# Third block's attention with tokens taken column by column, three key tiles a query block, both heads in one slot

## The chip, the cores and the metric

The kernel runs on one core of a Trainium2 chip. The metric is the device time of one execution in microseconds (us), lower is better. Five engines take part: TensorE (PE, with its weight loads PEld), VectorE (DVE), ScalarE (ACT), GpSimd (POOL) and SyncE (SP), which only issues DMAs here.

## The reference, cut to what matters

Three blocks run one after another on x of shape (1, 1024, 1024), in float32. The change lies in the third. Its attention sees the 1024 tokens as a grid of 16 rows by 64 columns, token t at row t // 64 and column t % 64. Each query attends to 8 rows by 16 columns around it, clipped at the edges, with a learned bias for each relative place; there are 8 heads of 64 channels.

```python
def neighbourhood_attention(q, k, v, rpb):
    rows = T // GRID_W                       # 16
    kh = min(MAX_KH, rows)                   # 8
    row_start = jnp.clip(row_ids - kh // 2, 0, rows - kh)
    col_start = jnp.clip(col_ids - KW // 2, 0, GRID_W - KW)      # KW 16, GRID_W 64
    ...
        s = jnp.einsum("bhwd,bhiwjd->bhwij", q_row, k_win).astype(jnp.float32) * scale
        s = s + bias.transpose(0, 2, 1, 3).astype(jnp.float32)[None]
        p = jax.nn.softmax(s.reshape(B, N_HEADS, GRID_W, kh * KW), axis=-1)
        return jnp.einsum("bhwij,bhiwjd->bhwd", p, v_win)

def third_block(...):
    proj = rms_norm(h, ln_g[l]) @ w_in[l] + b_in[l]
    glu_a, glu_b, z_conv, q, k, v, z_att = jnp.split(proj, cuts, axis=-1)
    y_conv = conformer_conv(glu_a, glu_b, ...)       # 31 taps along the tokens
    y_att = neighbourhood_attention(q, k, v, rpb[l])
    y_conv = grouped_rms_norm(y_conv, gn_conv_g[l], CONV_GROUPS) * jax.nn.silu(z_conv)
    y_att = grouped_rms_norm(y_att, gn_att_g[l], N_HEADS) * jax.nn.silu(z_att)
    h = h + jnp.concatenate([y_conv, y_att], axis=-1) @ w_out[l]
```

## The kernel before, in words

Activations are kept transposed: channels on the 128 partitions, the 1024 tokens (TOK) along the free axis. A product with a weight block is made of three matmuls (high parts by high, high by low, low by high); one block of 8 weight tiles on 1024 tokens is 48 matmuls (`feature_block`). GpSimd splits each weight block into its two parts ahead of TensorE, two blocks deep. Every result of TensorE goes through one of two PSUM slots `acc[0]` and `acc[1]` of 1024 numbers each, used in turn: `claim` makes TensorE wait until the slot's last reader has counted up `acc_free`.

The order on each engine is written out by hand; the engines meet only at semaphores. The attention of the third block is four units, one for each pair of heads (`near_tensor`, `near_scalar`, `near_vector`). In a unit TensorE makes q, turns v to token-major (`turn_tiles`), makes k and z, adds the rows of the pair before to the residual h (`near_rows`: eight products, each added to h by VectorE in `add_rows`), waits until both slots are free, and enters `att_tensor`. ScalarE takes v, q, k and z out of PSUM (`take`, L1831). VectorE carries the 31-tap convolution of four channel tiles beside it: 23 taps of 1024 tokens a unit (`conv_taps`, L1733), 12 before the gate of the last pair's output and 11 after `near_lo`. `near_hi` (L483 in `split_near`) stands in ScalarE's queue behind the takes of q and of v.

`att_tensor` runs over eight blocks p of 128 queries. Scores of a block are q times the keys that the block may see, for the two heads (sides) of the pair. VectorE adds the bias and takes the maximum (L813, in `att_vector`), ScalarE takes the exponential with its sum (L854), VectorE multiplies by the reciprocal (L823, L826), TensorE turns the probabilities (L720), ScalarE copies them back to SBUF (L864, and L870 for the fifth tile), TensorE multiplies them with v (L744), and ScalarE takes the outputs of four blocks at a time (L880, `take_outputs`). While the last blocks drain, TensorE starts on the next weight block (L407): three tiles, turn, value products, one tile, value products, and then its last four tiles, 24 matmuls.

Tokens lie row by row, so 128 queries are two grid rows, and their keys are 8 or 9 whole rows: 512 keys for blocks 0, 1, 6 and 7, and 576 for blocks 2 to 5. Each side takes a slot of its own, so a block of queries uses both. The bias table of a pair comes in five pieces through a ring of two (`load_chunk`, L1837).

The second block's window attention (`window_tensor`, `window_vector_steps`) uses the same `att_tensor` and `att_scalar` with `joint=True`: 256 keys for blocks 0 and 7 and 384 for blocks 1 to 6, both sides in the two halves of one slot, scores one block ahead (`ahead`), scores and probabilities in buffers of their own. It also has a sink, one more score in front of each row.

Of the kernel before, what the change touches and what calls it, by code (L numbers as in the profile page):

```python
# [129 lines left out]
NEAR_CHUNKS = 5  # L130
# [9 lines left out]
def keys_2(p):  # L140
# [15 lines left out]
def mixer_program(nc, x_t, blocks, n_blocks, params, consts, bias_1, bias_2, bias_3, sgu_rows, sgu_w, p_t,  # L156
                  out_t):

    with ExitStack() as ctx:
# [23 lines left out]
        def attention_buffers(base, kib, probs_kib, bias_kib, bias_width):  # L183
# [67 lines left out]
        window_scores = at("window_scores", 190, [P, 2, 2, 392])  # L251
# [11 lines left out]
            v_tok=at("near_v_tok", 148.625, [P, TT, P]), v_t=at("near_v_t", 156.625, [P, TOK]), scores=None,  # L263
# [67 lines left out]
        chunk_in = [sem("chunk_in0"), sem("chunk_in1")]  # L331
# [351 lines left out]
        def att_tensor(pe, t, a, keys, next_block=True, joint=False):  # L683
# [30 lines left out]
            def turn_probs(p):  # L714

                count = keys(p)[1]

                def turn(bank, side, c, at):
                    w = min(P, count - c * P)
                    return pe.transpose(turned[bank][0:w, at * P:(at + 1) * P],  # L720
                                        a.probs[:, p % 2, side, ahead + c * P:ahead + c * P + w], ident[:, :])
# [46 lines left out]
        def window_vector_steps(dve, t, ch, a, keys, n):  # L768
            ch.link(dve.tensor_copy(window_scores[:, :, :, 0],
                                    small[:, 40 + 2 * n:42 + 2 * n].unsqueeze(1).to_broadcast([P, 2, 2])))  # L770
            ch.sync()

            def take_scores(p):
                _, count, bias_at = keys(p)
                own, s = 8 * (p % 2), await_acc(dve, t)
                for side in range(2):
                    ins = dve.tensor_tensor_reduce(  # L777
                        out=window_scores[:, p % 2, side, 1:1 + count],
                        in0=acc[s][:, side * HALF:side * HALF + count],
                        in1=a.bias[:, side, bias_at:bias_at + count], scale=-1.0,  # L780
                        scalar=small[:, 40 + 2 * n + side:41 + 2 * n + side], op0=ALU.add, op1=ALU.min,
                        accum_out=small[:, own + side:own + side + 1])
                    ins.then_inc(acc_free[s] if side else first_scored, 1)

            def norm_probs(p):
                count, own = keys(p)[1], 8 * (p % 2)
                for side in range(2):
                    dve.wait_ge(exp_done, t.next("exp_done"))
                    ch.link(dve.reciprocal(small[:, own + 4 + side:own + 5 + side],
                                           small[:, own + 2 + side:own + 3 + side]))  # L790
                    ch.sync()
                    probs = a.probs[:, p % 2, side, 1:1 + count]
# [9 lines left out]
        def att_vector(dve, t, ch, a, keys, bias_of=None):  # L802
            def take_scores(p):
                _, count, bias_at = keys(p)
                if bias_of is None:
                    table = a.bias[:, :, bias_at:bias_at + count]
                else:
                    table = bias_of(p)[:, :, 0:count]
                slots = [await_acc(dve, t) for _ in range(2)]
                ch.link(dve.memset(small[:, 60:61], 3e38))  # L810
                ch.sync()
                for side, s in enumerate(slots):
                    dve.tensor_tensor_reduce(  # L813
                        out=a.probs[:, p % 2, side, 0:count] if a.scores is None else a.scores[:, side, 0:count],
                        in0=acc[s][:, 0:count], in1=table[:, side, :], scale=-1.0,
                        scalar=small[:, 60:61], op0=ALU.add, op1=ALU.min,
                        accum_out=small[:, side:side + 1]).then_inc(acc_free[s], 1)
# [16 lines left out]
        def att_scalar(act, t, ch, a, keys, joint=False, bias=None, load_bias=None):  # L834

            def exponential(p, side):
                count = keys(p)[1]
                if joint:
# [7 lines left out]
                    act.activation(a.probs[:, p % 2, side, 0:1 + count], window_scores[:, p % 2, side, 0:1 + count],  # L846
# [7 lines left out]
                act.activation(probs, probs if a.scores is None else a.scores[:, side, 0:count], ACT.Exp,  # L854
# [19 lines left out]
            def take_outputs(half):  # L874

                act.wait_ge(pv_done, t.next("pv_done"))
                if half == 0 and t.some("lo_ready"):
                    act.wait_ge(lo_ready, t.count("lo_ready"))
                func, offset = (ACT.Copy, 0.0) if bias is None else (ACT.Identity, bias)
                ch.link(act.activation(a.total[:, half * HALF:(half + 1) * HALF], att_out, func, bias=offset))  # L880

            for n in range(TT + 2):
                if n < TT:
                    for side in range(2):
                        exponential(n, side)
                    if load_bias is not None:
                        load_bias(n)
# [717 lines left out]
        def window_tensor(pe, t):  # L1605
# [3 lines left out]
            for n in range(HEAD_PAIRS):  # L1609
# [5 lines left out]
                att_tensor(pe, t, local, keys_2, next_block=n < HEAD_PAIRS - 1, joint=True)  # L1615
# [9 lines left out]
        def window_scalar(act, t, ch):  # L1625
# [3 lines left out]
            for n in range(HEAD_PAIRS):  # L1629
# [4 lines left out]
                att_scalar(act, t, ch, local, keys_2, joint=True)  # L1634
                take_total(act, t, ch, local, att2_hi[:, :])

        def window_vector(dve, t, ch):
# [4 lines left out]
            for n in range(HEAD_PAIRS):  # L1642
# [4 lines left out]
                window_vector_steps(dve, t, ch, local, keys_2, n)  # L1647
# [127 lines left out]
        def near_tensor(pe, t):  # L1775
            feature_block(pe, t)
            for n in range(HEAD_PAIRS):
# [9 lines left out]
                att_tensor(pe, t, near, keys_3)  # L1787
# [40 lines left out]
        def near_scalar(act, t, ch):  # L1828
# [4 lines left out]
            def load_chunk(pair, c):  # L1833
                p = (0, 1, 2, 6, 7)[c]
                _, count, at_ = keys_3(p)
                ring = (NEAR_CHUNKS * pair + c) % 2
                act.dma_start(near_bias[:, ring, :, 0:count], bias_3[pair][:, :, at_:at_ + count])\  # L1837
                   .then_inc(chunk_in[ring], 16)

            def load_bias(pair):  # L1840
                def load(n):
                    if n in (0, 1, 5):
                        load_chunk(pair, {0: 2, 1: 3, 5: 4}[n])
                    if n in (6, 7) and pair < HEAD_PAIRS - 1:
                        load_chunk(pair + 1, n - 6)
                return load
# [5 lines left out]
            load_chunk(0, 0)  # L1852
            load_chunk(0, 1)
            for n in range(HEAD_PAIRS):
                take(near.v_t[:, :], ACT.Copy)
# [3 lines left out]
                take(near.q_t[:, :], ACT.Identity, 0.125, q_bias[:, n:n + 1])  # L1859
# [3 lines left out]
                take(near.k_t[:, :], ACT.Identity, 1.0, col("pairs", PAIR_PAR * n + 1))  # L1863
# [3 lines left out]
                att_scalar(act, t, ch, near, keys_3, bias=col("pairs", PAIR_PAR * n + 2), load_bias=load_bias(n))  # L1867
# [79 lines left out]
        def near_vector(dve, t, ch):  # L1947
            def bias_of(pair):
                def table(p):
                    chunk = NEAR_CHUNKS * pair + (0, 1, 2, 2, 2, 2, 3, 4)[p]  # L1950
                    if p < 3 or p > 5:
                        dve.wait_ge(chunk_in[chunk % 2], 16 * (chunk // 2 + 1))
                    return near_bias[:, chunk % 2]
                return table

            conv_taps(dve, ch, (CONV_TILES - 1) * TAPS_BY_GLU, TAPS_EARLY)
            for n in range(HEAD_PAIRS):
# [13 lines left out]
                att_vector(dve, t, ch, near, keys_3, bias_of(n))  # L1971
# [271 lines left out]
def near_bias(rpb):  # L2243
# [3 lines left out]
    for p in (0, 1, 2, 6, 7):  # L2247
        first, count, at = BIAS_3[p]
        q, k = p * P + np.arange(P)[:, None], first + np.arange(count)[None, :]
        row, column, key_row, key_column = q // 64, q % 64, k // 64, k % 64  # L2250
# [99 lines left out]
```

## Time and profile before

| | |
|---|---|
| median of 3 runs | 3620.63 us (3619.98 to 3624.5) |
| profiled execution, its own time | 3623.64 us |
| its span, first to last instruction | 3621.9 us |
| mean granted TensorE clock | 0.985 |
| PE busy | 3478.8 us, 96% |
| PEld busy | 2772.5 us, 77% |
| DVE busy | 1728.9 us, 48% |
| ACT busy | 797.4 us, 22% |
| POOL busy | 1201.0 us, 33% |

Busy shares are of the span. The granted clock is 1.00 at 2.4 GHz and 0.50 at 1.2 GHz; a value between them is a mean. The third block's attention units lie between 3085 and 3452 us of the span, the second block's between 1878 and 2037 us. The chain that ended last is read back from the last instruction: each piece is what the next one waited for.

### The profile page before, as it was taken

The page shows a single profiled execution, that of the slowest core. Times are in us where ns is not written, and L with a number is a line of the kernel's source. Part 1 is how long each engine was busy: PE and PEld are TensorE (multiplying, and loading weights), DVE is VectorE, ACT ScalarE, POOL GpSimd, SP SyncE. Part 2 cuts the span into 40 slices and gives each one's busy share as a digit, 9 for nine tenths or more (in the row PEclk, how much of TensorE's full clock was granted, in tenths as well). Part 3 has the DMA queues.
Part 4 walks back from the last instruction along what each step waited for, and adds up shares of the span by engine and source line. Part 5 has one row for each costly group of instructions (what it writes and reads, how often), then busy time and mean ns, then how long its engine had stood idle before and what let it go on. Part 6 is the DMA issues. An engine that isn't in the chain of part 4 may idle for free.

```text
span 3621.9 us, 41941 instructions
## 1 busy us (share of the span) xinstructions
PE 3478.8 (96%) x16940; PEld 2772.5 (77%) x16940; DVE 1728.9 (48%) x2073; ACT 797.4 (22%) x1170; POOL 1201.0 (33%) x534
## 2 busy tenths in 40 slices
PE   7999999989999999989999999999999999999997
PEld 5767877778888888777876678888888868767675
DVE  4323433352323223588866642322322368888835
ACT  4433100020000000332234430000000141333452
POOL 2222344323433433333321134334333424222222
PEclk9999999999999999999999999999999999999998
DMA  2111211111111111122111011111111101111111
GB/s 95 39 36 38 93 47 46 47 35 47 46 52 46 46 52 46 35 66 81 59 34 33 23 41 47 52 46 46 52 46 58 47 18 60 59 60 58 44 35 64
DMA packets 52163, 178.96 MB, mean 49 GB/s; under 512 B 5728, under 2 KB 6368, under 8 KB 52064
## 3 DMA queue, kind: packets, MB, share of 16 engines
q1 hardware_dynamic: 38016, 138.43, 11.7%
q10 hardware_dynamic: 14048, 39.10, 3.2%
q8 instruction: 75, 1.23, 0.1%
q14 instruction: 24, 0.20, 0.0%
HBM read 172.79 MB, written 4.72 MB: 49 GB/s over the span
## 4 chain that ended last, share of the span: by engine, by line
PE 85%; DVE 8%; ACT 3%; issue 3%; POOL 1%; DMA 0%; ACTq 0%; DVEq 0%; POOLq 0%
PE acc L389 69%; PE acc L407 4%; PE acc L744 2%; PE acc L720 2%; PE acc L709 2%; PE acc L426 2%; DVE conv_slots L1733 1%; PE acc L473 1%; DVE rstd L618 1%; DVE normed L650 1%; DVE x_lo L488 0%; DVE h L897 0%; POOL w_lo L2060 0%; DVE window_scores L777 0%; PE acc L1355 0%
## 5 line engine op out<-in xcount | busy, mean ns | idle before, releaser
L2046 POOL TENSOR_TENSOR w_hi<-raw,zero 128x1024 fp32r<-128x1024 f32 x264 | 515.6, 1953 | 2365.2 <-PE acc L389 1663.1
L389 PE MATMUL acc<-x_hi,w_hi 128*128 128x512 f32 x2512 | 778.4, 391 | 5.7 <-POOL w_lo L2060 3.0
L389 PE MATMUL acc<-x_lo,w_hi 128*128 128x512 f32 x2512 | 774.2, 389 | 0.0
L389 PE MATMUL acc<-x_hi,w_lo 128*128 128x512 f32 x2512 | 774.0, 389 | 0.0
L2060 POOL TENSOR_TENSOR w_lo<-raw,w_hi 128x1024 fp32r<-128x1024 f32 x262 | 678.9, 2591 | 20.5
L897 DVE TENSOR_TENSOR h<-h,acc 128x1024 f32<-128x1024 f32 x312 | 380.7, 1221 | 554.9 <-PE acc L389 554.9
L389 PEld LDWEIGHTS acc<-x_hi,w_hi 128*128 128x128 f32 x2512 | 470.0, 188 | 106.7 <-POOL w_lo L2060 4.7
L389 PEld LDWEIGHTS acc<-x_lo,w_hi 128*128 128x128 f32 x2512 | 471.9, 188 | 98.7
L389 PEld LDWEIGHTS acc<-x_hi,w_lo 128*128 128x128 f32 x2512 | 471.8, 188 | 98.5
L1164 DVE TENSOR_TENSOR hid<-act_g,acc 128x1024 f32<-128x1024 f32 x44 | 53.7, 1221 | 570.7 <-PE acc L389 554.7
L483 ACT ACTIVATE hid_hi<-hid 128x1024 fp32r<-128x1024 f32 x44 | 46.7, 1061 | 909.2 <-DVE hid L1164 909.2
L1733 DVE SCALAR_TENSOR_TENSOR conv_slots<-conv_slots,par 128x1024 f32<-128x1024 f32 x120 | 227.8, 1898 | 4.1
L389 PE MATMUL acc<-hid_hi,w_hi 128*128 128x512 f32 x704 | 217.0, 389 | 0.7 <-DVE hid_lo L488 0.7
L389 PE MATMUL acc<-hid_lo,w_hi 128*128 128x512 f32 x704 | 216.7, 389 | 0.0
L389 PE MATMUL acc<-hid_hi,w_lo 128*128 128x512 f32 x704 | 216.7, 389 | 0.0
L488 DVE TENSOR_TENSOR hid_lo<-hid,hid_hi 128x1024 fp32r<-128x1024 f32 x44 | 138.2, 3140 | 49.9 <-ACT hid_hi L483 49.9
L389 PEld LDWEIGHTS acc<-hid_hi,w_hi 128*128 128x128 f32 x704 | 131.9, 188 | 28.5 <-DVE hid_lo L488 1.1
L389 PEld LDWEIGHTS acc<-hid_lo,w_hi 128*128 128x128 f32 x704 | 132.1, 188 | 27.5
L389 PEld LDWEIGHTS acc<-hid_hi,w_lo 128*128 128x128 f32 x704 | 132.1, 188 | 27.4
L1140 ACT ACTIVATE act_g<-acc 128x1024 f32<-128x1024 f32 x44 | 45.3, 1029 | 360.2 <-PE acc L389 360.1
L504 PEld LDWEIGHTS acc<-ident,mean_w 128*128 128x128 f32 x812 | 95.0, 194 | 21.0 <-issue 20.2
L504 PE MATMUL acc<-ident,mean_w 128*128 128x128 f32 x812 | 95.5, 278 | 16.2 <-DMA h<-x_t 16.2
(332 smaller groups left out, 4068.9 us busy)
## 6 DMA issues: line engine op xcount, KB each, us to landing
raw<-blocks SPq DMA_DIRECT2D x264, 512.0 KB, 3.4
near_bias<-bias ACTq DMA_DIRECT2D x16, 512.0 KB, 4.0
h<-x_t ACTq DMA_DIRECT2D x8, 512.0 KB, 8.2
h<-x_t ACTq DMA_DIRECT2D x1, 4096.0 KB, 15.5
q_past<-q_dram ACTq DMA_DIRECT2D x8, 512.0 KB, 5.6
w_own<-r_dram ACTq DMA_DIRECT2D x8, 512.0 KB, 6.5
out_t<-out_rows ACTq DMA_DIRECT2D x8, 512.0 KB, 3.0
band_bias<-bias ACTq DMA_DIRECT2D x4, 640.0 KB, 4.1
```

The costliest lines, as they stand in the source:

```text
L389: ins = pe.matmul(acc[s][:, c], w[:, slot, tile, :], part[:, c], start=(n == 0 and m == 0), stop=(n == last and m == 2))
L407: ins = pe.matmul(acc[s][:, c], w[:, slot, k, :], part[:, k, c], start=(k == 0 and m == 0), stop=(k == KT - 1 and m == 2))
L426: ins = pe.matmul(acc[accs[b]][:, c], w[:, slots[b], k, :], part[:, k, c], start=(k == 0 and m == 0), stop=(k == KT - 1 and m == 2))
L488: dve.tensor_tensor(lo, source, hi.bitcast(F32), ALU.subtract).then_inc(lo_ready, 1)
L504: pe.matmul(acc_all[:, 2 * TOK:2 * TOK + P], mean_w[:, :], ident[:, :], start=True, stop=True)
L709: ins = pe.matmul(acc[slots[side]][:, c0:c1], a.q_t[rows_of(side), p * P:(p + 1) * P], a.k_t[rows_of(side), first + c0:first + c1], start= ...
L720: return pe.transpose(turned[bank][0:w, at * P:(at + 1) * P], a.probs[:, p % 2, side, ahead + c * P:ahead + c * P + w], ident[:, :])
L744: ins = pe.matmul(att_out[rows_of(side), p % 4 * P:(p % 4 + 1) * P], a.v_tok[0:w, first // P + c, rows_of(side)], a.probs_t[0:w, p % 2, si ...
L897: dve.tensor_tensor(h[:, j, :], h[:, j, :], acc[s], ALU.add).then_inc(acc_free[s], 1)
L1733: ins = dve.scalar_tensor_tensor(out=out, in0=shifted, scalar=weight, in1=out, op0=ALU.mult, op1=ALU.add)
L2046: pool.tensor_tensor(hi, whole, nothing, ALU.add).then_inc(hi_split, 1)
L2060: pool.tensor_tensor(lo, whole, hi.bitcast(F32), ALU.subtract).then_inc(w_split, 1)
```

## The change

The tokens of q, k and v of the third block are put in column order (token at column * 16 + row) as ScalarE takes them out of PSUM: it reads the slot with a step of 64 numbers, 16 at a time, and writes without a gap. A block of 128 queries is then 8 grid columns of 16 rows, and the keys that it may see lie in three tiles (the tile itself and its neighbours): 384, or 256 at the two ends. Outputs are put back in row order when ScalarE takes them (`take_outputs` writes with a step of 64 numbers). Both sides share a slot, through the path of the window attention, with no sink (`sink=0`). The bias table of a pair is 896 columns for each side and comes in one load, issued by ScalarE after the pair before has ended. z is not reordered.

```diff
-BIAS_3 = [(0, 512, 0), (0, 512, 512)] + [((p - 2) * P, 576, 1024) for p in range(2, 6)] \
-    + [(512, 512, 1600), (512, 512, 2112)]
-N_BIAS_3 = 2624
+BIAS_3 = [(0, 256, 0)] + [((p - 1) * P, 384, 256) for p in range(1, TT - 1)] + [((TT - 2) * P, 256, 640)]
+N_BIAS_3 = 896
...
-            probs=at("near_probs", 152.625, [P, 2, 2, 640]), probs_t=at("near_probs_t", 162.625, [P, 2, 2, 5, P]),
-            total=at("near_att_sum", 172.625, [P, TOK]), bias=None)
-        near_bias = at("near_bias", 188.625, [P, 2, 2, 576])
+            scores=at("near_scores", 164.625, [P, 2, 2, 384]), probs=at("near_probs", 152.625, [P, 2, 2, 384]),
+            probs_t=at("near_probs_t", 158.625, [P, 2, 2, 3, P]), total=at("near_att_sum", 172.625, [P, TOK]),
+            bias=at("near_bias", 188.625, [P, 2, N_BIAS_3]))
...
-        def window_vector_steps(dve, t, ch, a, keys, n):
-            ch.link(dve.tensor_copy(window_scores[:, :, :, 0],
-                                    small[:, 40 + 2 * n:42 + 2 * n].unsqueeze(1).to_broadcast([P, 2, 2])))
-            ch.sync()
+        def joint_vector(dve, t, ch, a, keys, limits, sink):
...
                     ins = dve.tensor_tensor_reduce(
-                        out=window_scores[:, p % 2, side, 1:1 + count],
+                        out=a.scores[:, p % 2, side, sink:sink + count],
                         in0=acc[s][:, side * HALF:side * HALF + count],
                         in1=a.bias[:, side, bias_at:bias_at + count], scale=-1.0,
-                        scalar=small[:, 40 + 2 * n + side:41 + 2 * n + side], op0=ALU.add, op1=ALU.min,
+                        scalar=limits[side], op0=ALU.add, op1=ALU.min,
                         accum_out=small[:, own + side:own + side + 1])
...
+        def columns(x):
+
+            return x.rearrange("p (r c) -> p c r", r=GRID_ROWS)
...
-                ch.link(act.activation(a.total[:, half * HALF:(half + 1) * HALF], att_out, func, bias=offset))
+                if by_columns:
+                    n = HALF // GRID_ROWS
+                    out, source = columns(a.total[:, :])[:, n * half:n * half + n, :], att_out.rearrange(
+                        "p (c r) -> p c r", r=GRID_ROWS)
+                else:
+                    out, source = a.total[:, half * HALF:(half + 1) * HALF], att_out
+                ch.link(act.activation(out, source, func, bias=offset))
...
-                att_tensor(pe, t, near, keys_3)
+                att_tensor(pe, t, near, keys_3, joint=True)
...
-            def load_chunk(pair, c):
-                p = (0, 1, 2, 6, 7)[c]
-                _, count, at_ = keys_3(p)
-                ring = (NEAR_CHUNKS * pair + c) % 2
-                act.dma_start(near_bias[:, ring, :, 0:count], bias_3[pair][:, :, at_:at_ + count])\
-                   .then_inc(chunk_in[ring], 16)
+            def take_by_columns(dst, func, scale=1.0, bias=0.0):
+                s = await_acc(act, t)
+                act.activation(dst.rearrange("p (c r) -> p c r", r=GRID_ROWS), columns(acc[s]), func, scale=scale,
+                               bias=bias).then_inc(acc_free[s], 1)
 
             def load_bias(pair):
-                def load(n):
-                    if n in (0, 1, 5):
-                        load_chunk(pair, {0: 2, 1: 3, 5: 4}[n])
-                    if n in (6, 7) and pair < HEAD_PAIRS - 1:
-                        load_chunk(pair + 1, n - 6)
-                return load
+                act.dma_start(near.bias[:, :, :], bias_3[pair]).then_inc(bias_in, 16)
...
             for n in range(HEAD_PAIRS):
-                take(near.v_t[:, :], ACT.Copy)
+                take_by_columns(near.v_t[:, :], ACT.Copy)
...
-                take(near.q_t[:, :], ACT.Identity, 0.125, q_bias[:, n:n + 1])
+                take_by_columns(near.q_t[:, :], ACT.Identity, 0.125, q_bias[:, n:n + 1])
                 take(near.v_tok[:, :, :].rearrange("p a b -> p (a b)"), ACT.Copy)
...
-                take(near.k_t[:, :], ACT.Identity, 1.0, col("pairs", PAIR_PAR * n + 1))
+                take_by_columns(near.k_t[:, :], ACT.Identity, 1.0, col("pairs", PAIR_PAR * n + 1))
                 take(z_att[:, :], ACT.Silu, 1.0, col("pairs", PAIR_PAR * n + 3))
...
-                att_scalar(act, t, ch, near, keys_3, bias=col("pairs", PAIR_PAR * n + 2), load_bias=load_bias(n))
+                att_scalar(act, t, ch, near, keys_3, joint=True, bias=col("pairs", PAIR_PAR * n + 2), by_columns=True)
+                if n < HEAD_PAIRS - 1:
+                    load_bias(n + 1)
...
         def near_vector(dve, t, ch):
+            ch.link(dve.memset(small[:, 60:61], 3e38))
...
-                att_vector(dve, t, ch, near, keys_3, bias_of(n))
+                dve.wait_ge(bias_in, t.next("bias_in") * 16)
+                joint_vector(dve, t, ch, near, keys_3, [small[:, 60:61], small[:, 60:61]], 0)
```

The table of biases is laid out on the host for the new order, with query and key rows taken as index % 16 and columns as index // 16. Both first-block and second-block attention keep their order of work.

## Rows read from the trace of the kernel before

**Rows 1.** The page's chain that ended last, share of the span by engine.
```profile
PE 85%; DVE 8%; ACT 3%; issue 3%; POOL 1%; DMA 0%; ACTq 0%; DVEq 0%; POOLq 0%
```

**Rows 2.** Stretches: bounds, us, busy PE, PEld, DVE, ACT, POOL; PEclk, DMA share, GB/s.
```profile
1878.51:1911.18 32.67, 30.45 (x213) 20.93 (x214) 17.80 (x67) 17.92 (x51) 4.28 (x2) 1.00 0.10 29
3122.88:3167.07 44.19, 41.58 (x313) 29.14 (x314) 36.48 (x80) 25.00 (x56) 5.29 (x2) 0.96 0.25 74
3218.08:3262.19 44.11, 41.72 (x313) 29.24 (x314) 36.50 (x80) 23.84 (x55) 5.39 (x2) 0.96 0.25 74
3311.39:3356.39 45.00, 42.63 (x313) 29.71 (x314) 36.44 (x80) 23.85 (x55) 5.29 (x2) 0.92 0.25 73
3407.39:3452.18 44.79, 42.42 (x313) 29.71 (x314) 23.07 (x72) 25.13 (x56) 4.54 (x2) 0.92 0.17 50
```

**Rows 3.** Chain that ended last, third block's first unit: start us, us, what.
```profile
3122.88 1.15 PE acc L709 x4
...
3133.27 1.23 PE acc L709 x8
...
3136.81 1.23 PE acc L709 x8
...
3161.40 5.67 PE acc L407 x24
```

**Rows 4.** The same chain, second block's first unit.
```profile
1878.51 0.73 PE acc L697 x4
...
1888.05 0.84 PE acc L697 x4
...
1890.51 0.84 PE acc L697 x4
...
1905.52 5.66 PE acc L407 x24
```

**Rows 5.** Instruction groups of ScalarE: busy us, mean ns of one, idle before.
```profile
L864 ACT ACTIVATE near_probs_t<-acc 128x512 f32<-128x512 f32 x64 | 34.1, 583 | 14.6 <-PE acc L720 14.6
L846 ACT ACTIVATE local_probs<-window_scores,small 128x385 f32<-128x385 f32 x48 | 29.1, 614 | 0.0
L854 ACT ACTIVATE near_probs<-near_probs,small 128x576 f32<-128x576 f32 x32 | 24.6, 768 | 15.2 <-DVE small L813 15.2
L864 ACT ACTIVATE local_probs_t<-acc 128x384 f32<-128x384 f32 x48 | 21.4, 495 | 3.2 <-PE acc L720 2.5
L880 ACT ACTIVATE near_att_sum<-acc,par 128x512 f32<-128x512 f32 x8 | 5.5, 689 | 12.0 <-PE acc L744 12.0
L880 ACT ACTIVATE local_att_sum<-acc 128x512 f32<-128x512 f32 x8 | 4.8, 598 | 14.7 <-PE acc L744 14.7
L1831 ACT ACTIVATE near_q_t<-acc,q_bias 128x1024 f32<-128x1024 f32 x4 | 4.5, 1115 | 30.3 <-PE acc L389 30.3
L864 ACT ACTIVATE band_probs_t<-acc 128x128 f32<-128x128 f32 x8 | 1.7, 258 | 0.0
L1219 ACT ACTIVATE head_cols<-acc 128x64 f32<-128x64 f32 x1 | 0.2, 225 | 3.5 <-issue 3.5
```

**Rows 6.** Timeline around the second unit: start us, us, instruction, idle before and releaser.
```profile
3181.02 0.70 PE L389 MATMUL acc<-x_hi,w_hi 128*128 128x512 f32 x2 [0.42 <-ACT near_q_t L1831]
...
3182.77 1.87 DVE L488 TENSOR_TENSOR near_lo<-near_att_sum,near_hi 128x1024 fp32r<-128x1024 f32 x1 [4.44 <-ACT near_hi L483]
...
3207.64 0.73 PE L389 MATMUL acc<-near_hi,w_hi 128*128 128x512 f32 x2 [1.69 <-DVE h L897]
...
3218.08 1.13 PE L709 MATMUL acc<-near_k_t,near_q_t 64*128 64x512 f32 x4 [1.41 <-DVE h L897]
```

**Rows 7.** The page's DMA issues: KB each, us from issue to landing.
```profile
near_bias<-bias ACTq DMA_DIRECT2D x16, 512.0 KB, 4.0
```

**Rows 8.** Instruction groups of VectorE: a convolution tap.
```profile
L1733 DVE SCALAR_TENSOR_TENSOR conv_slots<-conv_slots,par 128x1024 f32<-128x1024 f32 x120 | 227.8, 1898 | 4.1
```

**Rows 9.** A stretch of 2 us in the first unit, columns as in rows 2.
```profile
3125.60:3127.60 2.00, 1.75 (x4) 0.53 (x4) 1.41 (x6) 0.99 (x4) 0.00 (x0) 0.50 0.27 31
```

More of the change, by code:

```diff
@@ L250, in mixer_program @@
         local.k_t = conv_in[:, 1, 4:TOK + 4]
[L251 removed]
+        local.scores = at("window_scores", 190, [P, 2, 2, 392])
         att2_hi = at("att2_hi", 161, [P, TOK], F32R)
@@ L678, in await_parts, with att_tensor @@
             pe.wait_ge(lo_ready, t.count("lo_ready"))
-        def att_tensor(pe, t, a, keys, next_block=True, joint=False):
+        def att_tensor(pe, t, a, keys, next_block=True, joint=False, sink=0):
             ahead = 1 if joint else 0
@@ L720, in turn @@
                     return pe.transpose(turned[bank][0:w, at * P:(at + 1) * P],
-                                        a.probs[:, p % 2, side, ahead + c * P:ahead + c * P + w], ident[:, :])
+                                        a.probs[:, p % 2, side, sink + c * P:sink + c * P + w], ident[:, :])
                 for side in range(2):
@@ L791, in norm_probs @@
                     ch.sync()
-                    probs = a.probs[:, p % 2, side, 1:1 + count]
+                    probs = a.probs[:, p % 2, side, sink:sink + count]
                     dve.tensor_scalar(probs, probs, small[:, own + 4 + side:own + 5 + side], None, ALU.mult)\
@@ L800, in window_vector_steps, with att_vector @@
                     norm_probs(p - 1)
-        def att_vector(dve, t, ch, a, keys, bias_of=None):
+        def att_vector(dve, t, ch, a, keys):
             def take_scores(p):
                 _, count, bias_at = keys(p)
[L805 to L808, printed above, removed]
                 slots = [await_acc(dve, t) for _ in range(2)]
@@ L813, in take_scores @@
                     dve.tensor_tensor_reduce(
-                        out=a.probs[:, p % 2, side, 0:count] if a.scores is None else a.scores[:, side, 0:count],
-                        in0=acc[s][:, 0:count], in1=table[:, side, :], scale=-1.0,
+                        out=a.scores[:, side, 0:count], in0=acc[s][:, 0:count],
+                        in1=a.bias[:, side, bias_at:bias_at + count], scale=-1.0,
                         scalar=small[:, 60:61], op0=ALU.add, op1=ALU.min,
@@ L832, in att_vector, with att_scalar @@
                     take_scores(p)
-        def att_scalar(act, t, ch, a, keys, joint=False, bias=None, load_bias=None):
+        def columns(x):
+            return x.rearrange("p (r c) -> p c r", r=GRID_ROWS)
+        def att_scalar(act, t, ch, a, keys, joint=False, sink=0, bias=None, by_columns=False):
             def exponential(p, side):
@@ L845, in exponential @@
                         act.wait_ge(acc_free[s], t.count(f"acc{s}"))
-                    act.activation(a.probs[:, p % 2, side, 0:1 + count], window_scores[:, p % 2, side, 0:1 + count],
+                    act.activation(a.probs[:, p % 2, side, 0:sink + count], a.scores[:, p % 2, side, 0:sink + count],
                                    ACT.Exp, scale=-1.0, bias=small[:, own + side:own + side + 1],
@@ L853, in exponential @@
                 probs = a.probs[:, p % 2, side, 0:count]
-                act.activation(probs, probs if a.scores is None else a.scores[:, side, 0:count], ACT.Exp,
+                act.activation(probs, a.scores[:, side, 0:count], ACT.Exp,
                                scale=-1.0, bias=small[:, side:side + 1],
@@ L1614, in window_tensor @@
                     await_all_taken(pe, t)
-                att_tensor(pe, t, local, keys_2, next_block=n < HEAD_PAIRS - 1, joint=True)
+                att_tensor(pe, t, local, keys_2, next_block=n < HEAD_PAIRS - 1, joint=True, sink=1)
             keep_clock(pe, 12)
@@ L1633, in window_scalar @@
                 pass_acc(t, KT)
-                att_scalar(act, t, ch, local, keys_2, joint=True)
+                att_scalar(act, t, ch, local, keys_2, joint=True, sink=1)
                 take_total(act, t, ch, local, att2_hi[:, :])
@@ L1646, in window_vector @@
                 dve.wait_ge(bias_in, t.next("bias_in") * 16)
-                window_vector_steps(dve, t, ch, local, keys_2, n)
+                ch.link(dve.tensor_copy(local.scores[:, :, :, 0],
+                                        small[:, 40 + 2 * n:42 + 2 * n].unsqueeze(1).to_broadcast([P, 2, 2])))
+                ch.sync()
+                joint_vector(dve, t, ch, local, keys_2, [small[:, 40 + 2 * n + side:41 + 2 * n + side] for side in range(2)],
+                             1)
                 split_lo(dve, t, local.total[:, :], att2_hi[:, :], att2_lo[:, :])
@@ L2246, in near_bias @@
     table = np.full((HEADS, P, N_BIAS_3), NEG, np.float32)
-    for p in (0, 1, 2, 6, 7):
+    for p in (0, 1, TT - 1):
         first, count, at = BIAS_3[p]
         q, k = p * P + np.arange(P)[:, None], first + np.arange(count)[None, :]
-        row, column, key_row, key_column = q // 64, q % 64, k // 64, k % 64
+        row, column, key_row, key_column = q % GRID_ROWS, q // GRID_ROWS, k % GRID_ROWS, k // GRID_ROWS
         row_start, column_start = np.clip(row - 4, 0, 8), np.clip(column - 8, 0, 48)
```

17 lines of the change are left out of this document (3 added, 14 removed).

## The prediction, made before the kernel was run

> **What bounds the kernel now.** I read the page first: the chain that ended last is 85% TensorE [rows 1], so what counts is what makes TensorE's queue longer or leaves it waiting. Then I read that chain in order of time for the third block's four attention units, and the busy time of the same stretches. A unit's attention starts when VectorE has added the last row of h, because TensorE waits for both slots [rows 6], and I end it where the weight block that is threaded into it ends. The first unit begins at 3122.88 and its last 24 matmuls end at 3161.40 + 5.67 = 3167.07 [rows 3]. The four stretches cut like this take 44.19, 44.11, 45.00 and 44.79 us, together 178.09 us [rows 2]. In them TensorE is busy 41.6 to 42.6 us, so the reader sees a stretch that is almost all matmul, transposes and weight changes, and whose length goes with the number of key columns. In steady state a block of queries takes 3136.81 - 3133.27 = 3.54 us there [rows 3].
>
> The useful find is that the trace already holds the attention that the change puts in this place. The second block's units run `att_tensor` and `att_scalar` with both heads in one slot, 256 keys at the ends and 384 between, eight query blocks, the same threaded weight block. Those are the counts of the new `BIAS_3`. The first unit, from its first score matmul at 1878.51 to the end of the same 24 matmuls at 1905.52 + 5.66 = 1911.18, takes 32.67 us [rows 2, 4], and one block of queries 1890.51 - 1888.05 = 2.46 us [rows 4]. It also begins like a unit of the third block does: all slots are free, the last add of h just ended.
>
> **The change part by part.**
>
> *Fewer keys, one slot.* By the code a pair's eight blocks see 4 x 512 + 4 x 576 = 4352 keys a side before and 2 x 256 + 6 x 384 = 2816 after, 35% fewer. The half-filled fifth tile, its transposes and its copy (L870) go. On ScalarE an exponential falls from 0.768 to 0.614 us and a copy of turned probabilities from 0.583 to 0.495 us [rows 5], so a block sheds 2 x 0.154 + 2 x 0.088 = 0.48 us, and the fifth-tile copy on top. VectorE is busy 36.5 us of a stretch before, with taps of the convolution in its tail, and 17.8 us in the window unit, which has none [rows 2]; nothing on it or on ScalarE stands above the window unit's pace. I don't add these up, because they overlap: I take the whole window stretch as the price of the new one. 178.09 - 4 x 32.67 = 178.09 - 130.68 = **47.4 us less**.
>
> The sink is one more score in a row of 385 and a small copy hidden beside the first scores; leaving it out is worth 16 numbers of ScalarE, some 0.01 us a unit. The `memset` of the limit moves out of the blocks into the start, where VectorE waits for TensorE: nothing.
>
> *Outputs.* In the window unit the first `take_outputs` is on the chain. With a bias operand it takes 0.689 instead of 0.598 us [rows 5]: 4 x 0.09 = **0.4 us more**. The second one is followed only by the square, which is needed after the 24 matmuls (5.67 us); it is hidden.
>
> *Reads and writes with a step of 64 numbers.* v, q and k are read so from PSUM, outputs written so to SBUF. Which of them lie on the path: the take of q does, twice over. TensorE waits for it before k's block (0.42 us already), and `near_hi` stands behind it in ScalarE's queue, then `near_lo`, eleven taps, the first adds of h, and TensorE's third row product, which waits 1.69 us for such an add [rows 6]. So each extra us of q's take moves both. The take of v has q's whole weight block as cover, the take of k has z's. The first half of the outputs is on the path, 512 numbers. Together 1024 + 512 numbers a unit, 6144 in four.
> What does a stepped read cost? The trace has one short example: L1219 reads 64 numbers a partition from PSUM, in runs of 8 with exactly this step of 64, in 0.225 us. Copies without a step take 0.258 us for 128 numbers and 0.583 us for 512, so 0.846 ns a number and 0.204 us for 64 [rows 5]. The difference, 0.021 us, is either noise or 0.33 ns a number. Bounds: nothing below (a step can't speed up a read), 6144 x 0.33 ns = 2.0 us by that row, and, since no row shows a stepped write, 6144 x 0.85 = 5.2 us if every number took twice its time. I take the middle of the nearest row's two readings, **1.0 us more**.
> The Trainium skill, page Advanced Engine Details and Errata, section Memory Cachelines, speaks against the change here: SBUF has lines of 16 bytes and PSUM of 8, and accesses that go to another line each time pay a penalty. It gives no size for ScalarE. By it every number of these reads and writes is penalised, and the sum would go to the doubled case below or past it; L1219, the only row with such a step, doesn't show a doubling.
>
> *Bias table.* Five issues of ScalarE in a unit become one. One load of 128 x 2 x 896 numbers is 896 KB; by the 4.0 us of a 512 KB load [rows 7] some 7 us. It is issued when a unit ends and needed after four weight blocks, some 40 us later. Hidden; without that cover it would cost up to 7 us in three units. The issue stands before the square of the outputs in ScalarE's queue, under the 24 matmuls. Less DMA traffic frees nothing that anyone waits for.
>
> *What the earlier end runs into.* After the attention VectorE has 12 taps, the gate, then waits 4.44 us for `near_hi` [rows 6]. This wait ends by TensorE's q block, so VectorE's late chain (11 taps, adds) is tied to TensorE and moves up with it as long as those 4.44 us hold. VectorE's own attention work shortens with TensorE's in the window unit, so the slack changes little. GpSimd has two weight blocks ready as before. Nothing late in the unit appears to be left behind.
>
> **The sum.** -47.4 + 0.4 + 1.0 = -46.0 us. Against the profiled execution: span 3621.9 to 3575.9, its time 3623.64 to 3577.6. The median of the runs is 3.0 us under that execution's time, so I forecast 3620.63 - 46.0 = **3574.6 us**, 1.3% less. A no-change measurement of this kernel can't be told within about 0.2%, 7 us.
>
> **The rivals.**
>
> *The clock dips as it does today.* The third block's units have a mean granted clock of 0.96, 0.96, 0.92 and 0.92, with stretches at 0.50 (1.2 GHz) just after the first scores [rows 2, 9]. The window unit stayed at 1.00 (2.4 GHz). If the new units keep the dips, at most 0.06 x 44.5 = 2.7 us of full-speed work is lost in each, 10.7 us in all: up to 3585.3. For it: the same place and engine. Against it: the window unit also begins with small matmuls and a wait, and kept its clock.
>
> *Steps cost double.* 5.2 us in place of 1.0: 3578.8. For it: no row shows the write, and the skill's rule. Against it: L1219.
>
> *VectorE falls behind.* Taps run at 1.9 us on average [rows 8], unevenly as GpSimd works beside them. If the new timing costs one tap in each of three units after `near_lo`, the sum is 5.7 us worse: 3580.3. For it: TensorE already waits there. Against: 4.44 us of slack before.
>
> *Slower than before.* One mechanism could do it: stepped access at many times the plain price. It acts on 1536 path numbers a unit, whose gain is 46.9 / 4 = 11.7 us; it decides from 11.7 / 1.536 = 7.6 ns more a number, nine times the plain 0.85 ns. At 10 ns: 6144 x 10 = 61 us more and 47 less, 3635 us. Nothing in the rows is near that.
>
> *The change doesn't do what it says:* the code sets the counts, and the window unit shows this path at work, so I give it nothing of its own.
>
> **How the numbers follow.** The forecast 0.70; clock dips 0.12; double steps 0.10; VectorE behind 0.05; slower 0.02; other 0.01. Low end: the forecast without the 1.0 us of steps, without the dip-like waits for the adds (some 2 us), and with the runs' scatter of 2 us below: 3569. High end: dips in full, 3585. All cases but the last are faster by far over 7 us: faster 0.96, same 0.02, slower 0.02.
>
> **What would show it right or wrong.** In the profile after: four stretches from the first score to the end of the 24 matmuls at 32.7 to 33.5 us, a block pace of 2.46 us, the granted clock in them near 1.00; takes of v, q and k near 1.03 to 1.5 us and the outputs near 0.69 to 0.9 us; the table's landing long before the first bias add; the span outside these stretches unchanged within 3 us, with `near_lo` still waiting for `near_hi`. The prediction is wrong if the takes are above 2 us, if the first scores run at half clock again, or if the wait for adds of h at `near_rows` grows.

## The result, and the profile after

The changed kernel takes 3578.48 us (median, 3575.78 to 3578.84), the kernel before beside it 3621.03 us: a ratio of 0.9877, 95% interval 0.9865 to 0.9888, so 42.6 us or 1.2% faster. The forecast was 3574.6 us with a range of 3569 to 3585. Between the two profiled executions the difference is 3623.64 - 3578.16 = 45.5 us, against a forecast sum of 46.0. The median of the kernel before moves by some 2 us from one set of runs to the next (3621.03 here, 3621.31 and 3623.52 below), so a difference of medians is good to a few us, and the small terms are read from the stretches of the profiles.

Stretches of the changed kernel: the four attention units from the first score matmul to the end of the 24 matmuls, cut as in [rows 2], with the same columns.

```profile
3123.51:3156.70 33.19, 30.51 (x213) 20.98 (x214) 29.33 (x72) 20.18 (x52) 5.91 (x2) 1.00 0.13 45
3207.59:3240.79 33.20, 30.50 (x213) 20.94 (x214) 29.47 (x72) 18.96 (x51) 5.76 (x2) 1.00 0.14 45
3289.93:3323.16 33.23, 31.51 (x213) 21.58 (x214) 29.50 (x72) 18.86 (x51) 5.68 (x2) 0.95 0.13 44
3374.06:3407.26 33.20, 30.50 (x213) 20.93 (x214) 16.36 (x64) 20.23 (x52) 4.27 (x2) 1.00 0.06 17
```

They sum to 132.82 us where they were 178.09 [rows 2]: 45.3 us of the 45.5 are gained here. Read the first number of each row: all four are 0.5 us above the 32.67 us of the window unit that served as the model.

The changed kernel's chain that ended last, in the first unit (start us, us, what), beside [rows 3] and [rows 4]:

```profile
3123.51 0.72 PE acc L695 x4
...
3130.59 0.84 PE acc L695 x4
3131.43 0.81 PE acc L718 x6
3132.24 0.81 PE acc L742 x12
3133.04 0.85 PE acc L695 x4
...
3138.01 1.14 ACT near_att_sum L881
...
3151.01 5.68 PE acc L405 x24
```

The take of the outputs in the window unit, from the same chain as [rows 4]:

```profile
1893.01 0.60 ACT local_att_sum L880
```

A block of queries takes 3133.04 - 3130.59 = 2.45 us, and its three pieces (scores, turned probabilities, value products) are all TensorE's: the steady part is a chain of matmuls, 35% shorter in columns and 31% shorter in time. Both units reach the take of the outputs 14.50 us after their first score; the take is the one piece that is clearly longer than in the window unit, 1.14 against 0.60 us on the chain.

ScalarE's instruction groups in the changed kernel, beside [rows 5]:

```profile
L841 ACT ACTIVATE near_probs<-near_scores,small 128x384 f32<-128x384 f32 x48 | 28.9, 609 | 0.0
...
L881 ACT ACTIVATE near_att_sum<-acc,par 128x512 f32<-128x512 f32 x8 | 9.3, 1167 | 16.4 <-PE acc L742 16.4
...
L1838 ACT ACTIVATE near_q_t<-acc,q_bias 128x1024 f32<-128x1024 f32 x4 | 4.5, 1114 | 30.3 <-PE acc L387 30.3
```

The take of q reads with a step of 64 numbers in 1.114 us, as long as it took without a step (1.115); the takes of v (1.024 us) and k (1.118) didn't move either. The output take writes with that step and went from 0.689 to 1.167 us.

Between the units almost nothing moved. The two rows are the stretch after the first unit and the one after the second:

```profile
3156.70:3207.59 50.89, 47.46 (x204) 36.87 (x203) 44.36 (x27) 13.55 (x12) 22.04 (x8) 1.00 0.13 42
3240.79:3289.93 49.14, 47.36 (x205) 36.80 (x204) 42.50 (x27) 13.55 (x12) 21.40 (x8) 1.00 0.14 44
```

Before, the same stretches, from 3167.07 to 3218.08 and from 3262.19 to 3311.39, were 51.01 and 49.20 us. The timeline around the second unit shows the same waits as [rows 6]:

```profile
3170.64 0.70 PE L387 MATMUL acc<-x_hi,w_hi 128*128 128x512 f32 x2 [0.42 <-ACT near_q_t L1838]
...
3172.39 1.87 DVE L486 TENSOR_TENSOR near_lo<-near_att_sum,near_hi 128x1024 fp32r<-128x1024 f32 x1 [4.06 <-ACT near_hi L481]
...
3197.25 0.74 PE L387 MATMUL acc<-near_hi,w_hi 128*128 128x512 f32 x2 [1.69 <-DVE h L896]
```

VectorE's slack before `near_lo` is 4.06 us (4.44 before), and the wait for the adds of h is 1.69 us as before. The bias table lands 4.4 to 4.8 us after its issue, some 50 us ahead of its use.

### The profile page after: what moved, and what is told of

Read it like the earlier page. It is cut to its first block, busy times and chain, and to the rows that moved or that the text cites. A ratio compares the mean times of both kernels' runs of the same rounds, so it can differ in the third digit from the quotient of the medians.

```text
span 3576.4 us, 41017 instructions
## 1 busy us (share of the span) xinstructions
PE 3432.6 (96%) x16540; PEld 2738.6 (77%) x16540; DVE 1701.7 (48%) x2042; ACT 777.6 (22%) x1154; POOL 1202.8 (34%) x534
## 4 chain that ended last, share of the span: by engine, by line
PE 85%; DVE 8%; ACT 3%; issue 3%; POOL 1%; DMA 0%; ACTq 0%; DVEq 0%; POOLq 0%
PE acc L387 70%; PE acc L405 4%; PE acc L742 2%; PE acc L718 2%; PE acc L424 1%; DVE conv_slots L1736 1%; PE acc L471 1%; DVE rstd L616 1%; PE acc L695 1%; DVE normed L648 1%; PE acc L707 1%; DVE x_lo L486 0%; DVE h L896 0%; POOL w_lo L2051 0%; DVE window_scores L772 0%
```

## The experiments

### The write with a step: plain_outputs and step_on_read

In `plain_outputs` the outputs are written without a step and so stay in column order: the kernel leaves out the step that puts them back in row order, and its result is not the reference's:

```diff
-                if by_columns:
+                if False:
```

> The changed kernel with the outputs written without a step (they stay in column order; everything else as changed). Theory A, the write with a step of 64 numbers doubles the copy and its first half is on the path: the output take falls from 1.16 to 0.69 us, each of the four attention stretches from 33.2 to 32.75 us, in all 1.8 us less than the changed kernel. Theory B, the step costs an instruction but its time is hidden: the take falls, the stretches stay at 33.2 us.

`step_on_read` computes what the changed kernel does, with the two loops of the copy swapped:

```diff
-                    out, source = columns(a.total[:, :])[:, n * half:n * half + n, :], att_out.rearrange(
-                        "p (c r) -> p c r", r=GRID_ROWS)
+                    out = a.total[:, :].rearrange("p (r c) -> p r c", r=GRID_ROWS)[:, :, n * half:n * half + n]
+                    source = att_out.rearrange("p (c r) -> p r c", r=GRID_ROWS)
```

> The changed kernel with the same reordering of outputs, but the loops of the copy swapped: it reads PSUM with a step of 16 numbers and writes runs of 32. Theory A, on ScalarE only writes pay for a step, reads from PSUM don't: the take is 0.69 us and the stretches are 32.75 us, 1.8 us in all, as with plain outputs. Theory B, any stepped side pays: the take stays at 1.1 us and above, stretches at 33.2 us.

The output take of `step_on_read`, from the instructions of its tile (duration ns least/median/most, first and last start):

```profile
L881 ACT ACTIVATE near_att_sum<-acc,par x8: 687/688/691, 3137.8 to 3399.8; 128x512 f32<-128x512 f32 x8
```

and two of its attention stretches:

```profile
3123.30:3156.10 32.80, 30.50 (x213) 20.97 (x214) 29.33 (x72) 19.28 (x52) 5.89 (x2) 1.00 0.14 45
3206.99:3239.77 32.78, 30.48 (x213) 20.93 (x214) 29.44 (x72) 18.09 (x51) 5.76 (x2) 1.00 0.14 45
```

The four stretches are 32.80, 32.78, 32.79 and 32.82 us, together 131.19, which is 1.6 us less than the changed kernel's 132.82; in `plain_outputs` the take is 0.690 us and the stretches are 32.8 us each. Theory A holds in both, with 1.6 us in place of its 1.8: on this take the step costs only where it is written, the cost is 0.4 us a unit on the path, and the swapped loops avoid it at no price that shows. Medians are 3576.01 us (`step_on_read`) and 3576.40 us (`plain_outputs`), each 0.9876 of the kernel before, interval 0.9859 to 0.9892; a gain of 1.6 us is too small for the medians to show, and rests on the stretches.

### What a step costs: write_steps

Nine copies of ScalarE stand in front of the kernel, in this order: plain; written with steps of 2, 4, 8, 16 and 64 numbers (`cut`); read with steps of 2, 4 and 64.

```diff
+            one(act.activation(dst[:, 0:HALF], half, ACT.Copy))
+            one(act.activation(cut(dst, 512)[:, 0:1, :], runs(half, 512), ACT.Copy))
+            one(act.activation(cut(dst, 256)[:, 0:2, :], runs(half, 256), ACT.Copy))
...
+            one(act.activation(cut(dst, 16)[:, 0:32, :], runs(half, 16), ACT.Copy))
+            one(act.activation(runs(dst[:, 0:HALF], 512), cut(flat, 512)[:, 0:1, :], ACT.Copy))
...
```

> The changed kernel with nine copies of ScalarE and six of VectorE in front, each of 512 numbers a partition, in SBUF: plain; written with a step of 2, 4, 8, 16 and 64 numbers; read with a step of 2, 4 and 64 (VectorE: plain, written with 2, 4 and 64, read with 4 and 64). They add nothing to the result. Theory A, ScalarE pays about twice the time a number for any write that leaves no two numbers side by side, the same at step 2 as at 64, and nothing for reads: writes 1.05 us, reads 0.62 us. Theory B, the price grows with the step: about nothing at 2, all at 64. For VectorE no theory beyond the same two.

Its timeline on ScalarE, lines in the order given above:

```profile
11.53 0.63 ACT L2103 ACTIVATE probe_a<-h 128x512 f32<-128x512 f32 x1
12.19 0.67 ACT L2104 ACTIVATE probe_a<-h 128x512 f32<-128x512 f32 x1
12.89 1.13 ACT L2105 ACTIVATE probe_a<-h 128x512 f32<-128x512 f32 x1
14.05 1.14 ACT L2106 ACTIVATE probe_a<-h 128x512 f32<-128x512 f32 x1
15.22 1.07 ACT L2107 ACTIVATE probe_a<-h 128x512 f32<-128x512 f32 x1
16.33 1.10 ACT L2108 ACTIVATE probe_a<-h 128x512 f32<-128x512 f32 x1
17.46 0.68 ACT L2109 ACTIVATE probe_a<-h 128x512 f32<-128x512 f32 x1
18.17 1.15 ACT L2110 ACTIVATE probe_a<-h 128x512 f32<-128x512 f32 x1
19.36 1.08 ACT L2111 ACTIVATE probe_a<-h 128x512 f32<-128x512 f32 x1
```

Neither theory holds. A step of 2 is nearly free (0.67 us against 0.63), a step of 4 costs the whole price (1.13 us, 0.97 ns more a number), and from there to 64 it doesn't grow. Each form was timed once. The writes ran beside GpSimd's work, but so did the plain copy, and the last two reads ran after it. And reads pay too, when the source is SBUF: 0.68, 1.15 and 1.08 us at steps 2, 4 and 64. So what is free is ScalarE's stepped read from PSUM, at 64 numbers (the takes of q, k and v) and at 16 (`step_on_read`), and not reads as such. The kernel's one execution here took 3583.68 us; it serves only for these copies.

The six copies of VectorE say less. Its reads from SBUF with steps of 4 and 64 took 0.629 and 0.626 us; no plain copy ran at the same moment, and the nearest row, the scaling of 512 probabilities in the kernel before (L826), takes 0.486 us, so a stepped read may cost it some 0.14 us. The plain copy took 1.51 us and its stepped writes 2.20 to 2.54 us, but these four ran while GpSimd split weight blocks (8.31 to 17.31 us of the span), so the price of a stepped write of VectorE stays open.

### How much is the columns, how much the shared slot: two_slots

Column order and three tiles of keys, with each side in a slot of its own, no scores ahead, and VectorE's old order of steps:

```diff
-                att_tensor(pe, t, near, keys_3, joint=True)
+                att_tensor(pe, t, near, keys_3)
...
-                joint_vector(dve, t, ch, near, keys_3, [small[:, 60:61], small[:, 60:61]], 0)
+                att_vector(dve, t, ch, near, keys_3)
```

with `joint=True` gone from `att_scalar` as well, and one buffer of scores in place of two.

> Column order and three tiles of keys, but each side in its own slot, with the old order of VectorE's steps. Theory A, most of the gain is the fewer columns, and the shared slot with scores one block ahead is worth a part: steady pace of a block near 2.8 us instead of 2.46 (3.54 before the change), half-clock dips after the first scores as before the change, stretches near 37.5 us, in all 17 us slower than the changed kernel, near 3595 us. Theory B, the columns are everything: stretches at 33.2 us, same time as the changed kernel. Theory C, the shared slot is most of it: pace above 3.1 us, stretches above 40 us.

```profile
3126.82:3162.49 35.67, 31.98 (x213) 21.73 (x214) 30.26 (x79) 20.00 (x52) 5.24 (x2) 0.95 0.12 42
3213.48:3250.13 36.65, 33.23 (x213) 22.24 (x214) 30.26 (x79) 18.83 (x51) 4.28 (x2) 0.91 0.12 41
3299.31:3335.73 36.42, 33.11 (x213) 22.46 (x214) 30.25 (x79) 18.83 (x51) 5.24 (x2) 0.91 0.12 41
3386.71:3423.46 36.75, 33.26 (x213) 22.36 (x214) 19.61 (x72) 20.09 (x52) 4.27 (x2) 0.91 0.05 15
```

Its stretches sum to 145.49 us. Taken in this order, the fewer columns are worth 178.09 - 145.49 = 32.6 us and the shared slot, with the order of steps that comes with it, 145.49 - 132.82 = 12.7 us. The slot, the scores ahead and VectorE's order were not tried one by one. Its median of 3591.29 us (0.9915 of the kernel before, interval 0.9898 to 0.9931) is 13 us over the changed kernel's. Theory A came nearest, with the loop's pace (2.8 us, measured 2.68) and the half-clock dips; it had the share of the slot at 17 us. The chain of this kernel shows what binds its later blocks:

```profile
3136.30 0.62 DVE near_scores L804
...
3136.96 0.72 ACT near_probs L849 x2
3137.68 0.02 issue
3137.70 0.17 DVE small L814
3137.87 0.02 issue
3137.90 0.42 DVE near_probs L817
...
3138.98 0.62 DVE near_scores L804
```

From one block's bias add to the next is 3138.98 - 3136.30 = 2.68 us, and no matmul is in it: VectorE won't add the next block's bias before it has scaled this block's probabilities, and these wait for ScalarE. With 4352 key columns TensorE's steady blocks were slow enough to hide that loop (3.54 us, all matmuls [rows 3]); with 2816 they aren't, and the shared slot with scores a block ahead is what lets VectorE go on (2.45 us, TensorE again).

The loop is only about half of the 12.7 us. The other part is the clock: it fell in all four units here (0.95, 0.91, 0.91, 0.91), with the same key columns as the changed kernel, in which it fell in one. The chain of the second unit, where the granted clock is 0.50 from 3217.5 to 3221.5 us:

```profile
3218.02 1.65 PE acc L707 x4
3219.67 1.47 PE acc L718 x6
3221.15 1.05 PE acc L742 x8
3222.20 1.52 PE acc L707 x4
```

At full clock the same pieces take about 0.85, 0.81, 0.59 and 0.85 us. From the second to the fourth block's bias add the four units take 6.24, 7.22, 6.91 and 7.33 us, where two rounds of the loop would take 5.36. That is an estimate, with the loop's pace for what full clock would leave: 6.3 of the 12.7 us go with the slow clock, and 6.4 us, 1.6 a unit, are left for the loop. So it is the shared slot and its order, not the fewer columns, that took most of the dips away; how they do so, no run shows.

### Is the take of q on the path: q_twice

```diff
-                take_by_columns(near.q_t[:, :], ACT.Identity, 0.125, q_bias[:, n:n + 1])
+                s = await_acc(act, t)
+                for again in range(2):
+                    ins = act.activation(near.q_t[:, :].rearrange("p (c r) -> p c r", r=GRID_ROWS), columns(acc[s]),
+                                         ACT.Identity, scale=0.125, bias=q_bias[:, n:n + 1])
...
```

> The changed kernel with the take of q done twice, one after the other, some 1.2 us more before the slot comes free. Theory A, the take of q is on the path in all four units (before k's block for TensorE, and before near_hi for VectorE's late chain): 4 x 1.2 = 4.8 us slower than the changed kernel, all of it in the stretches between the attentions. Theory B, the wait is swallowed by other slack: under 1.5 us.

```profile
3158.67:3210.72 52.05, 47.48 (x205) 36.85 (x204) 44.36 (x27) 14.65 (x13) 22.05 (x8) 1.00 0.13 41
...
3243.90:3294.21 50.31, 47.38 (x205) 36.80 (x204) 42.51 (x27) 14.66 (x13) 21.39 (x8) 1.00 0.13 43
```

The stretches between attentions are 52.05, 50.31 and 52.04 us where the changed kernel has 50.89, 49.14 and 50.90: 1.14 to 1.17 us more each, and ahead of the first unit TensorE waits 1.57 us for q's take in place of 0.42. That is 4.6 us for four takes (4.8 expected); the median is 3583.94 us, 5.5 us over the changed kernel's. The take of q was rightly counted as path; that its stepped read is free is read from its 1.114 us.

### Two versions beyond: hi_first and no_slot_wait

`hi_first` is `step_on_read` with `near_hi` ahead of q's take:

```diff
+                if n:
+                    split_near(act, t)
                 take_by_columns(near.q_t[:, :], ACT.Identity, 0.125, q_bias[:, n:n + 1])
                 take(near.v_tok[:, :, :].rearrange("p a b -> p (a b)"), ACT.Copy)
-                if n:
-                    split_near(act, t)
```

> step_on_read with split_near before the take of q in ScalarE's queue. Theory A, near_lo starts some 2.9 us earlier and the wait of TensorE for the adds of h in the second and fourth unit goes: the stretches between attentions fall from 50.9 to 49.2 us in two of three, 3.4 us less than step_on_read. Theory B, the taps that start earlier run more beside GpSimd's work and give it back: under 1 us.

`no_slot_wait` adds to it:

```diff
                 if n:
                     near_rows(pe, t)
-                await_all_taken(pe, t)
+                else:
+                    await_all_taken(pe, t)
```

> hi_first, and from the second unit on TensorE no longer waits for both slots to be free before the scores (the claims of the slots remain). Theory A, the first bias add of VectorE starts 0.1 to 0.2 us after the last add of h in place of 0.9 us: 0.7 us in three units, 2.1 us less than hi_first, some 7 us less than the changed kernel. Theory B, something else holds the first scores: no change against hi_first.

> The changed kernel as it is, on the chip and beside the runs of this call: 3578 us, with stretches of 33.2 us as in its first profile. If the two profiles differ by more than 1 us somewhere outside the attention units, such a difference is no effect of the change.

A stretch between two attentions and the third unit, of `hi_first`:

```profile
3155.93:3205.02 49.09, 47.35 (x206) 36.76 (x204) 43.53 (x27) 13.64 (x12) 22.04 (x8) 1.00 0.13 43
...
3287.08:3319.87 32.79, 30.49 (x213) 20.97 (x214) 29.45 (x72) 18.09 (x51) 5.67 (x2) 1.00 0.13 45
```

of `no_slot_wait`:

```profile
3153.80:3201.53 47.73, 47.31 (x205) 36.77 (x204) 42.34 (x26) 13.62 (x12) 22.15 (x8) 1.00 0.13 44
3201.53:3235.00 33.47, 30.65 (x214) 20.83 (x214) 30.66 (x73) 18.18 (x51) 5.76 (x2) 1.00 0.14 44
...
3282.89:3317.80 34.91, 32.09 (x214) 21.57 (x214) 30.73 (x73) 18.19 (x51) 5.67 (x2) 0.95 0.13 42
```

and of `changed_again`:

```profile
3287.49:3320.71 33.22, 31.50 (x213) 21.57 (x214) 29.47 (x72) 18.87 (x51) 5.66 (x2) 0.95 0.14 44
```

`hi_first` went as theory A said: stretches between attentions of 49.09, 49.25 and 49.24 us, 3.4 us less than `step_on_read` from the first score to the end of the fourth unit (278.78 against 282.13 us). Its median of 3572.45 us is 5.6 us under the 3578.03 us of `changed_again` beside it; 0.986 of the kernel before, interval 0.9843 to 0.9876. One caution: in `changed_again` the first of the two long waits for the adds of h did not come (82.31 us from the first unit's start to the second's, against 84.08 in the first profile of the same kernel), so the late taps cost 1.7 or 3.5 us from one execution to the next, and in its one profile `hi_first` is free of that. By its own expectation, then, `changed_again` shows that a difference of some 1.7 us between the attentions is no effect of the change.

`no_slot_wait` missed. Scores start 1.4 us earlier (47.73 against 49.09 us), but the attention stretch then takes 33.47 in place of 32.81 us, which leaves 0.7 us a unit as forecast; and in the third unit the granted clock fell to half for some 3 us (0.95 over the stretch), which took 34.91 us in place of 33.47 and ate most of the rest. In all 278.16 against 278.78 us, and 3571.89 us in the median, 0.6 under `hi_first`: within what a run can tell, no change. It is the lowest of all, 0.9858 of the kernel before (0.9842 to 0.9875).

## Why the prediction was right, point by point

*The model for the sum.* Taking the window unit whole as the price of the new unit was right to 0.13 us a unit once outputs are written plainly (32.80 against 32.67 us), and that remainder is mostly the bias operand of the take, 0.09 us by [rows 5]. This is the main term, 47.4 us, and it carried the forecast.

*Fewer keys, one slot.* Right as one term. The split into 32.6 and 12.7 us wasn't in the forecast, and by [rows 4] alone could not have been told; nor was it said that half of the second part is a clock that stays up.

*Outputs and steps.* This term was mis-sized: 0.4 + 1.0 = 1.4 us were forecast for outputs, their bias operand and all steps; the stretches show 132.82 - 130.68 = 2.1 us, all of it at the output take. The measured take of 1.167 us also lies outside the 0.69 to 0.9 us that the forecast gave as its sign. The middle of one row's two readings was the wrong shape of answer: reads from PSUM cost 0.0 and the writes the full double price. L1219, the row that I leaned on, reads PSUM; it says nothing about a write to SBUF, and the text had noted that no row showed one. The doubled bound applied to the 512 written path numbers alone, 4 x 512 x 0.85 ns = 1.7 us, would have met the 1.6 us that `step_on_read` took back.

*Which takes are on the path.* Right, shown by `q_twice`. The bias table, the memset, the sink and ScalarE's issues are hidden, as said: the three stretches between the units are 0.1 us shorter each, the part after the last unit is 0.6 us shorter, and the first unit starts 0.6 us later, which it doesn't in `changed_again` (3122.82 us against 3122.88 before). The table's load took 4.6 us and not the 7 of the forecast, with no effect on the time.

*The clock.* The forecast had it at 1.00, and named first scores at half clock as a sign against it. Three units kept 1.00; the third had 0.95 in both profiles of the changed kernel, with its third block's scores at half clock (1.65 us where they take 0.85), so that sign did show in one unit. It cost next to nothing: 33.23 us, 0.03 more than the others. The dip lies in the first blocks, where the other units wait for VectorE, and the slow matmuls just filled that wait. The rival priced such dips at 2.7 us of full-speed work a unit (its "at most" is a mean; a unit at 0.92 would lose 3.6), which was too much where another engine sets the pace. In `no_slot_wait` the dip came later in its unit, on matmuls that set the pace (1.43, 1.05 and 1.44 us where 1.08, 0.59 and 0.85 are usual), and cost 1.4 us; in `two_slots` it came in all four units and cost up to 2 us in one, by the estimate above. That it cost the changed kernel nothing is in part luck of its place. What brings it in one unit and not in its neighbours stays open: in `plain_outputs`, `step_on_read`, `q_twice`, `hi_first` and `write_steps` the third unit kept 1.00 too.

*VectorE behind.* The slack held (4.06 us), and the wait for the adds stayed at 1.69 us, where it comes at all.

*Slower than before.* The dearest stepped access seen cost 0.97 ns more a number, where this rival needed 7.6 (worked out from 46.9 us, which the terms make 47.0; nothing hangs on it).

*The base.* 45.5 us were gained between the profiled executions against 46.0 in the sum. So 0.5 of the 3.9 us between the forecast and the measured median is the sum. The rest is the base: the forecast took 3.0 us off the profiled execution, as the median before lay, and the changed kernel's median lies 0.3 us above its profiled execution. The medians differ by 42.6 us in the first set of runs and by 45.5 in the one with `changed_again`, so this part is within what a few runs scatter.

## What to carry to other kernels

Look for a stage of the same program that already runs the shape that a change would give, cut it from the trace at the same two instructions, and use its length whole; correct only for what differs, and for each correction find a row on the same side of the same memory. When a stage gets fewer columns, ask which loop it had hidden: here that loop, VectorE to ScalarE and back in 2.68 us, and the clock that fell beside it would have kept 12.7 of the 45.3 us back without the shared slot. Look at the clock of each variant before a whole difference is put down to its chain. If ScalarE must permute on the way from PSUM to SBUF, let it read with the step and write in runs.

## What the runs showed of the hardware

ScalarE copies 512 float32 numbers a partition in 0.63 us from SBUF to SBUF. A step of 2 numbers on either side leaves it at 0.67 to 0.68, a step of 4 or more makes it 1.07 to 1.15, the same for reads and writes, and a step of 64 (or 16) on a PSUM source adds nothing (0.688 us for 512 numbers with a bias, 1.114 us for 1024). The Trainium skill, page Advanced Engine Details and Errata, section Memory Cachelines, has SBUF lines of 16 bytes that want two hits each; 2 numbers apart there are two to a line and 4 apart one, so these times agree with it. Its PSUM lines of 8 bytes are told of matmuls, which no run here tries; ScalarE's reads of PSUM did not pay.

VectorE read SBUF with steps of 4 and 64 in 0.63 us for 512 numbers; ScalarE takes 1.15 and 1.08 us for the same reads. Both were timed once (`write_steps`).

A stretch with TensorE at 1.2 GHz for some 3 us (granted clock 0.95 over the unit) cost 0.03 us in one kernel and 1.4 us in another. In the first it fell on blocks that VectorE paces at full clock, in the second on blocks that TensorE paces. With both heads in slots of their own the clock fell in every unit, with the shared slot in at most one.
